# A two-layer mixer and a second block in one kernel: GpSimd's powers for the next layer spread over nine feed-forward units, and two weights' low parts put behind the attention's

## What is computed

```python
for layer in range(2):
    xn = rms_norm(h, attn_norm_g[layer])
    u_ssm, u_g, v_g, q, k, v = split(xn @ w_in[layer])
    y_ssm  = s5_mixer(u_ssm, ...)          # complex-diagonal state space model, GELU, GLU
    y_sgu  = spatial_gating(u_g, v_g, ...)
    y_diff = diff_attention(q, k, v, ...)  # differential attention, rms_norm at its end
    h = h + concatenate([y_ssm, y_sgu, y_diff]) @ w_out[layer]
    xn = rms_norm(h, ffn_norm_g[layer])
    h = h + (gelu(gate) * val) @ w_down[layer]   # gate, val: xn @ w_up after a causal conv of width 3
```

## Time and profile before

| | |
|---|---|
| median of 3 executions | 1001.0 us |
| lowest and highest | 999.23 and 1001.94 us |
| the profiled execution | 999.57 us |
| its span in the trace | 997.8 us |
| TensorE busy | 966.1 us |
| VectorE busy | 701.2 us |
| ScalarE busy | 547.1 us |
| GpSimd busy | 252.9 us |

### The profile page before, as it was taken

One profiled execution on the slowest core, in us unless ns is written; L12 is line 12 of the kernel. 1 busy time (PEld: TensorE's weight loads), 2 busy tenths in 40 slices (PEclk: granted clock), 3 DMA queues, 4 the chain that ended last, 5 costly groups with the idle time before them and its releaser, 6 DMA issues.

```text
span 997.8 us, 15915 instructions
## 1 busy us (share of the span) xinstructions
PE 966.1 (97%) x6214; PEld 848.8 (85%) x6214; DVE 701.2 (70%) x1072; ACT 547.1 (55%) x898; POOL 252.9 (25%) x196
## 2 busy tenths in 40 slices
PE   6989999999999999999999999999999999999997
PEld 4868789999888887889999988999877789888886
DVE  6998557798954688657677856547676755666785
ACT  7645546665654655645576545545354454555723
POOL 4890102688400021102525300003112300000030
PEclk9999999999999999999999999999999999999999
DMA  7622355655565553247666664665544545754462
GB/s 295 213 84 85 88 186 178 189 179 177 172 188 166 168 171 127 64 138 232 190 191 189 188 192 149 205 209 177 169 148 148 148 142 158 218 152 156 148 190 85
DMA packets 48474, 165.97 MB, mean 166 GB/s; under 512 B 6544, under 2 KB 7056, under 8 KB 48400
## 3 DMA queue, kind: packets, MB, share of 16 engines
q1 hardware_dynamic: 48400, 164.95, 53.2%
HBM read 162.83 MB, written 1.05 MB: 164 GB/s over the span
## 4 chain that ended last, share of the span: by engine, by line
PE 81%; DVE 13%; ACT 2%; issue 2%; POOL 1%; DMA 1%; SPq 0%; DVEq 0%; POOLq 0%; ACTq 0%
PE PJ L583 13%; PE PJ L585 12%; PE PJ L584 12%; PE PJ L576 9%; PE PJ L577 9%; PE PJ L578 9%; DVE wlo L1670 5%; PE PJ L539 2%; PE PJ L541 2%; PE PJ L540 2%; DMA raw<-weights_in 1%; PE T L1013 1%; PE PJ L700 1%; PE T L1004 1%; ACT whi L1072 1%
## 5 line engine op out<-in xcount | busy, mean ns | idle before, releaser
L1670 DVE TENSOR_TENSOR wlo<-raw,whi 128x1024 fp32r<-128x1024 f32 x294 | 375.2, 1308 | 92.1 <-ACT whi L1072 89.8
L1072 ACT ACTIVATE whi<-raw 128x1024 fp32r<-128x1024 f32 x294 | 303.3, 1062 | 67.8 <-DMA raw<-weights_in 61.3
L576 PE MATMUL PJ<-xthb,whi 128*128 128x256 f32 x864 | 243.2, 281 | 4.5 <-DVE wlo L1670 3.7
L578 PE MATMUL PJ<-xthb,wlo 128*128 128x256 f32 x864 | 242.1, 280 | 0.0
L577 PE MATMUL PJ<-xtlb,whi 128*128 128x256 f32 x864 | 242.0, 280 | 0.0
L583 PE MATMUL PJ<-whi,xthb 128*128 128x512 f32 (+1 forms) x432 | 175.2, 406 | 5.7 <-DVE wlo L1670 3.6
L576 PEld LDWEIGHTS PJ<-xthb,whi 128*128 128x128 f32 x864 | 163.1, 189 | 6.4 <-issue 6.2
L585 PE MATMUL PJ<-whi,xtlb 128*128 128x512 f32 (+1 forms) x432 | 167.8, 388 | 0.0
L584 PE MATMUL PJ<-wlo,xthb 128*128 128x512 f32 (+1 forms) x432 | 167.8, 388 | 0.0
L577 PEld LDWEIGHTS PJ<-xtlb,whi 128*128 128x128 f32 x864 | 163.1, 189 | 0.2
L578 PEld LDWEIGHTS PJ<-xthb,wlo 128*128 128x128 f32 x864 | 163.1, 189 | 0.0
(11 more groups left out here) (398 smaller groups left out, 1382.9 us busy)
## 6 DMA issues: line engine op xcount, KB each, us to landing
raw<-weights_in SPq DMA_DIRECT2D x294, 512.0 KB, 3.5
rt<-bmerge_in SPq DMA_DIRECT2D x6, 256.0 KB, 4.4
xres<-x_in SPq DMA_DIRECT2D x2, 512.0 KB, 5.5
xn<-mem_in SPq DMA_DIRECT2D x2, 512.0 KB, 5.7
y_out<-xn SPq DMA_DIRECT2D x4, 256.0 KB, 2.4
rowv<-rows_in SPq DMA_DIRECT2D x1, 576.0 KB, 10.2
ptmp<-bexp_in SPq DMA_DIRECT2D x2, 256.0 KB, 6.1
cex<-cexp_in SPq DMA_DIRECT2D x2, 256.0 KB, 8.2
```

The costliest lines, as they stand in the source:

```text
L576: pe.matmul(o, a, xh[:, k, :], start=(first and f % 2 == 0), stop=False, skip_group_check=True)
L578: m = pe.matmul(o, b, xh[:, k, :], start=False, stop=last, skip_group_check=True)
L1072: act.activation(whi[:, p % HIGHS, :], raw[:, p % LOADS, :], ACT.Copy).then_inc(hi_ready, 1)
L1670: dve.tensor_tensor(wlo[:, p % LOADS, :], raw[:, p % LOADS, :], whi[:, p % HIGHS, :].bitcast(F32), ALU.subtract).then_inc(lo_ready, 1)
```

## The change

There are two edits. GpSimd's input powers are cut into four steps, and the output powers into six, and these are put behind the products of units 2 to 5 and 7 to 9, with the folded coefficients behind unit 6. The two copies and the decay table stand behind unit 10. VectorE's turns move from behind unit 8's htl to behind the last unit's, and ScalarE's phase table from ahead of the last unit's hth to behind it. In the first layer only, two low parts move from ahead of the attention's `mix_low` calls to behind them.

```diff
--- before.py
+++ after.py
@@ -378,18 +378,21 @@
                 link(eng.tensor_tensor(t, i1, k1, ALU.mult))
                 link(eng.tensor_tensor(o, o, t, ALU.add))
 
-        def output_powers(eng, link, l, c, tmp):
+        def output_powers(eng, link, l, c, tmp, steps=(0, 1, 2)):
 
             ar, ai = (wide(apw[:, c, 1:STEP + 1, 8 * l:8 * l + 8].rearrange("p t s -> p s t"), 32, 3) for c in range(2))
             cr, nci = (wide(gpw[:, c, :, 0, :], STEP, 2) for c in range(2))
             t = tmp.rearrange("p (s t h) -> p s t h", s=ST, t=STEP)
             i0, k0, i1, k1, op = ((cr, ar, nci, ai, ALU.add), (nci, ar, cr, ai, ALU.subtract))[c]
             o = gpw[:, c, :, 1:STEP + 1, :]
-            link(eng.tensor_tensor(o, i0, k0, ALU.mult), False)
-            link(eng.tensor_tensor(t, i1, k1, ALU.mult))
-            link(eng.tensor_tensor(o, o, t, op))
-
-        def input_powers(eng, link, l, c, x, tmp):
+            if 0 in steps:
+                link(eng.tensor_tensor(o, i0, k0, ALU.mult), False)
+            if 1 in steps:
+                link(eng.tensor_tensor(t, i1, k1, ALU.mult))
+            if 2 in steps:
+                link(eng.tensor_tensor(o, o, t, op))
+
+        def input_powers(eng, link, l, c, x, tmp, steps=(0, 1)):
 
             ar, ai = (wide(apw[:, k, 1:STEP, 8 * l:8 * l + 8].rearrange("p t s -> p s t"), 32, 3) for k in range(2))
             br, bi = (wide(bex[:, k, :, :], STEP - 1, 2) for k in range(2))
@@ -397,11 +400,13 @@
             t = tmp[:, 0:ST * 96].rearrange("p (s t h) -> p s t h", s=ST, t=STEP - 1)
             o = xv[:, :, 1:STEP, :]
             i1, k1, op = (bi, ai, ALU.subtract) if c == 0 else (br, ai, ALU.add)
-            link(eng.tensor_copy(xv[:, :, 0, :], bex[:, c, :, :]), False)
-            link(eng.tensor_tensor(o, br if c == 0 else bi, ar, ALU.mult), False)
-            link(eng.tensor_tensor(t, i1, k1, ALU.mult))
-            link(eng.tensor_tensor(o, o, t, op))
-            eng.sem_inc(sem("xpow_ready"), 1)
+            if 0 in steps:
+                link(eng.tensor_copy(xv[:, :, 0, :], bex[:, c, :, :]), False)
+                link(eng.tensor_tensor(o, br if c == 0 else bi, ar, ALU.mult), False)
+            if 1 in steps:
+                link(eng.tensor_tensor(t, i1, k1, ALU.mult))
+                link(eng.tensor_tensor(o, o, t, op))
+                eng.sem_inc(sem("xpow_ready"), 1)
 
 
         @block.sync
@@ -1326,7 +1331,7 @@
                             hi_upto(end_pair(f"up{l}_{j}") + 5)
                     if j < UNITS:
                         unit_gelu(j)
-                    if l + 1 < LAYERS and j == UNITS - 1:
+                    if l + 1 < LAYERS and j == UNITS:
                         phase_tables(act, l + 1)
                 n_next = 2 if l + 1 < LAYERS else 5
                 if l + 1 == LAYERS:
@@ -1597,16 +1602,21 @@
                     if l + 1 == LAYERS and j == 6:
                         norm_rstd(4)
                     if l + 1 < LAYERS:
-                        if j in (3, 4):
+                        if j == 2:
                             pool.wait_ge(sem("bex_ready"), l + 2)
-                            input_powers(pool, link, l + 1, j - 3, x_tile(j - 3), ptmp)
-                        if j == 5:
+                        if 2 <= j < 6:
+                            input_powers(pool, link, l + 1, j // 2 - 1, x_tile(j // 2 - 1), ptmp, (j % 2,))
+                        if j == 6:
                             folded(l + 1)
-                        if j in (6, 7):
-                            output_powers(pool, link, l + 1, j - 6, ptmp)
+                        if j == 7:
+                            output_powers(pool, link, l + 1, 0, ptmp, (0, 1))
                         if j == 8:
+                            output_powers(pool, link, l + 1, 0, ptmp, (2,))
+                            output_powers(pool, link, l + 1, 1, ptmp, (0,))
+                        if j == 9:
+                            output_powers(pool, link, l + 1, 1, ptmp, (1, 2))
+                        if j == 10:
                             replicate_inputs(l + 1)
-                        if j == 10:
                             decay_table(pool, link, l + 1)
                             pool.sem_inc(sem("decay_ready"), 1)
 
@@ -1972,7 +1982,7 @@
                 lo_upto(s0 + 23)
                 diff_sums(1)
                 diff_norm(1)
-                lo_upto(s0 + 26)
+                lo_upto(s0 + (26 if l else 24))
                 mix_low(4, S1[:, :], 3)
                 mix_low(6, S0[:, :], 4)
 
@@ -2029,7 +2039,7 @@
                         lo_upto(end_pair(f"up{l}_{j}") + 4)
                     if j > 0:
                         unit_lo(j - 1)
-                    if l + 1 < LAYERS and j == 9:
+                    if l + 1 < LAYERS and j == UNITS:
                         dve.wait_ge(sem("gpow_ready"), 4)
                         phase_turns(dve, link, 1)
                     if l + 1 == LAYERS and j == 9:
```

## The result

The changed kernel takes 1001.29 us (median of 12 runs, 999.78 to 1003.78) where the kernel before, timed beside it, takes 999.88 (12 runs, 999.22 to 1002.19). The ratio of the two is 1.0016, with an interval of 1.0008 to 1.0023: slower by about 1.6 us, which lies within the 0.3% that the forecast called no change. The profiled execution has a span of 998.8 us, against 997.8. Most lines of the changed kernel stand five to ten further down (1072 has become 1077, 1670 is 1680, 1859 is 1869, 1297 is 1302, 649 is 654, 583 is 588), and this execution is 0.5 us ahead of the one before from its first rows on.

A forecast was written before the change was run, and what follows sets the result against it. TensorE, busy 966.1 of 997.8 us, was taken to bound the kernel. The terms -1.5 - 3.35 + 2.45 + 2.6 gave +0.2 us; with the shown runs' median of 1001.0 the forecast was 1001.2 us, range 998.0 to 1004.6.

The forecast's parts named there:

- Its own signs of being wrong: Wrong if a new wait is missing or over 3.5 us, or the granted clock falls at either.
- the wait for xtlb: TensorE's wait for the attention output's low half at the first mixing end was to be under 0.3 us.
- the short wait at the sixth pair: First down projection: a short TensorE wait after the fifth pair's 2.7 us, with ScalarE's table ahead of its release.
- Mixing end, -1.5: First mixing end: one low part instead of three ahead of the attention parts releases TensorE 1.5 us earlier (1.2 to 1.6).
- Units 8 and 9, -3.35: First layer's feed-forward units: moved GpSimd powers lie beside VectorE's taps, removing the whole 3.35 us loss.
- the bound of -3.0: Units 8 and 9: the gain is only 3.0 us if one low part is still caught.
- the third rival: Units 8 and 9: powers never slowed the low parts, so 3.35 us stays; +3.5 us, 1004.5 us, 3 in 100.
- Transposes, +2.45: Second eight input transposes behind unit 6: TensorE waits for GpSimd's late powers, a new 2.45 us stall (2.0 to 2.8).
- The rival by which the engines take turns after every instruction: VectorE and GpSimd alternate, so the transposes' stall is 0.9 instead of 2.45 us; 999.7 us, 12 in 100.
- the rival with both waits hidden: Transposes and turns cost the path nothing: -4.85 us, 996.2 us, 6 in 100.
- Phase table and turns, +2.6: First down projection: later turns and phase table delay TensorE's fifth and sixth pairs, +2.6 us (2.1 to 3.2).
- TensorE's clock falls in the new stalls: At transposes and down projection, 1.65 us lost per fall: one gives 1002.8 us (10 in 100), two 1004.4 (4 in 100).

The follow-up runs named there:

- the mixing end alone: The kernel before with only VectorE's low parts reordered at the first mixing end: 999.04 us, ratio 0.9990.
- the kernel filled at both: The changed kernel with TensorE's waits at the input transposes and the down projection filled with transposes of the identity: 1000.52 us, ratio 1.0005.
- the powers alone: The changed kernel with the first mixing end's low parts ordered as in the kernel before: 1003.75 us, ratio 1.0038.
- the kernel without the transposes' wait: The changed kernel with the last two instructions of GpSimd's second set of input powers issued in unit 4, not unit 5: 998.87 us, ratio 0.9989.
- The third set of the changed kernel: The changed kernel timed and profiled a third time, unchanged, beside the kernel before: 1000.46 us, ratio 1.0015.
- the positions mended: The changed kernel with those input powers finished in unit 4 and the splits ahead of turns and phase tables: 994.46 and 995.15 us.
- the kernel filled at the down projection: The changed kernel with sixteen transposes of the identity between the down projection's fourth and fifth pairs: 1000.91 us, ratio 1.0012.

## Why the prediction was right, point by point

**The forecast of 1001.2 us** met 1001.29, partly by luck. Its sum was +0.2 us and 1.4 to 1.6 was measured; the level it was put on, the median of three runs at 1001.0, was 1.1 over the 999.88 of twelve runs.

**Its own signs of being wrong.** One of them came true. By its last sentence the prediction is wrong if the granted clock falls at either new wait, and it fell at the down projection (0.52 and 0.62 in the windows above). Of the rest, the wait for xtlb was met (0.44 us on the weight load, none in the matmul's own row), the new waits are 2.13 and 2.35 where about 2.4 and 2.7 were named, and the short wait at the sixth pair is missing in this profile. So the terms and the places were right, and the picture of a kernel that keeps its clock was not.

**Mixing end, -1.5.** The weight load moved from 120.20 to 118.16, of which 0.54 is this execution's head start: -1.50. The edit alone was timed at 1.0 and 0.9.

**Units 8 and 9, -3.35.** Measured -3.25 and -0.10. The 0.10 had nothing to do with the powers: the second profile of before and the mixing end alone have 11.20 and 11.21 us at that step. The reason given was half right. The powers don't lie beside the taps alone: two low parts are still caught (238.26), more than the one that the bound of -3.0 allowed for, and yet TensorE waits for none, because the loss on VectorE is 2.6 us (4.92 - 2 x 1.16) and not 8.6. With the steps at 11.20 us the third rival (3 in 100) is out.

**Transposes, +2.45.** Measured +2.33, with the released instruction and the engine as named. Moving the two powers one unit up took 2.7 us out. The rival by which the engines take turns after every instruction (12 in 100) is out too: gtd of unit 5 took 5.55 us (209.11), and the powers ended at 218.03. So is the rival with both waits hidden (6 in 100).

**Phase table and turns, +2.6.** Without a fall of the clock 2.64 was measured (the kernel filled at both; 16.68 - 14.05 = 2.63 in the powers alone). The chain was as described, down to the short second wait at the sixth pair (0.48), which is ScalarE's chain. Putting the splits ahead took it out whole. In the changed kernel's own profile the term is 3.62, since the clock fell.

**The sum** of the four as measured is -1.50 - 3.35 + 2.33 + 2.64 = +0.12 us, with the clock kept up (+0.22 without the 0.10 above). The kernel with both waits filled is that case: 1000.52 against 1000.13, a ratio of 1.0005 whose interval takes in +0.12 us.

**What was mis-sized is the rival "TensorE's clock falls in the new stalls"**, at 10 in 100 for one fall and 4 in 100 for two. The price was right where the transposes' fall is concerned: 1.65 forecast, 1.55 and 1.60 measured; the other costs 0.98. The chance was wrong: four profiled executions had both waits bare, and three of them show one fall and the fourth both. With 3 in 6 and 4 in 5 as the chances, the mean cost is 0.5 x 1.6 + 0.8 x 1.0 = 1.6 us, and 0.12 + 1.6 = 1.7 is what the three timings of the changed kernel show (1.6, 2.3 and 1.5 by the ratios; by the means of the single times 1.1, 2.1 and 1.6). The forecast of two falls has a slip besides: 0.2 + 2 x 1.65 is 3.5, not 3.4. The step that failed was the sentence that the point of decision "lies between" a wait of 1.5 and one of 3.15 us, followed by a forecast as if 2.45 lay below it. There is no sharp point in these traces: 2.11 and 2.40 us drew a fall and 2.15 and 2.36 drew none. Nor did the very wait that I had taken as proof of a fall always draw one. 12 of the 14 profiles have it with 3.14 to 3.16 us; the clock fell behind it in nine and kept up in three. In two of those three it fell only behind a second wait of 1.8 us, 5 us later. The third is the kernel without the transposes' wait, whose timeline of TensorE and windows have:

```profile
71.69 0.47 PE L588 MATMUL PJ<-whi,xthb 128*128 128x512 f32 x1 [3.14 <-DVE wlo L1680]
...
76.49 0.47 PE L588 MATMUL PJ<-whi,xthb 128*128 128x512 f32 x1 [1.79 <-DVE wlo L1680]
```

```profile
70.00:72.00 2.00, 0.31 (x1) 0.30 (x2) 2.00 (x2) 0.49 (x1) 1.92 (x2) 1.00 0.02 6
72.00:74.00 2.00, 2.00 (x10) 1.65 (x9) 1.90 (x5) 0.14 (x1) 1.80 (x2) 1.00 0.00 0
```

The first matmul took 0.47 us and not 0.77, and the clock stayed at 1.00. By the Trainium skill (TensorE: Matmul & The Clock Gate, Part 1, "What's actually happening") the monitor's phase is not tied to the kernel's start and the cold stretch differs from run to run; the traces fit that, as the same code at the same wait went both ways.

The price of 1.65 us was met by luck too. It is the clock time lost in a stretch where the fall cost the path nothing: from that matmul to the attention's transposes (their weight load at 116.20 in before) it is 45.59 us in before, with a fall, and 117.28 - 71.69 = 45.59 in the kernel above, without one, because TensorE then waits 1.79 us for the next low part instead. Behind the transposes nothing covers a fall, and there the price was 1.55 and 1.60 us.

The single times are weaker evidence. The third set of the changed kernel has seven times from 1000.23 to 1000.81 us, at a mean granted clock of 0.995, and four from 1002.45 to 1003.80, at 0.992 or 0.993, with nothing between; the gap of 1.64 us is near the price of the transposes' fall. But the widest gaps in the other two sets are 0.8 and 1.3 us, and one execution at 0.992 took 999.78 us. So this is argued from one set, not shown.

**Where the gain went.** The change took out 4.85 us of waiting and put 4.97 back at two places that it had itself made late, and these two drew 1.6 us more in clock. The idea was sound and two of its positions were not: with the positions mended the same edits are worth 4.5 us. That is a little under the 4.85, and the marks show where some of it stays: the step over the transposes is 13.06 us there and not 12.96, and the three units behind it take 11.31, 11.30 and 11.31, so 0.4 us go to the slower pitch of the last section.

## What to carry to other kernels

Before work is spread over earlier or later slots, list for each piece who reads it first and which long instruction now stands ahead of it; one slot earlier for two instructions, and splits ahead of a wait and not behind it, made the difference between +1.6 and -4.5 us here. A wait of 2 us or more on TensorE should be priced with a fall of its clock at even odds or worse (7 of 11 here, and 9 of 12 at 3.15 us), not left out because the likeliest execution lacks it. And a fall has its full price only where TensorE would not have waited anyway: the one at 70 us cost nothing here. Where the wait can't be removed, harmless transposes in it kept the clock in all three profiled executions, and cost nothing.

## What the runs showed of the hardware

**A fall is a matter of chance, and transposes count against it.** 11 bare waits of 2.1 to 2.4 us drew 7 falls, 3 filled ones none, and the timings of the kernel filled at both are lower than the changed kernel's by 1.8 us in their own set (ratios 1.0005 and 1.0023). If 7 in 11 were the chance with the filling too, three without a fall would come about once in 20 times. Length counts for something, but not sharply: 12 waits of 1.47 to 1.79 us near 59 us drew no fall, and in the kernel filled at the down projection one of 3.16 us drew none where one of 1.83 us, 5 us later, was followed by one. The Trainium skill (TensorE: Matmul & The Clock Gate, Part 4) says that transposes don't count as busy time in the same way; three executions and one timing speak against that for holding a clock that is already up. Raising it with transposes was not tried.

**Two pitches at full clock.** At a granted clock of 1.00 a unit of 96 matmuls takes either 11.20 or 11.31 us (116.7 or 117.8 ns for each). The slower one appeared in the first layer behind the transposes (units 8 to 10) in all four profiles in which the moved powers leave no wait there, but not in the two of before and the one of the mixing end alone, which have no wait there either (before has it in one step of its first profile). It appeared in all ten units of the second layer in three of 14 profiles, one of them of the changed kernel, which has 11.20 in its other two, and in the first step of the first layer in six of the 14. What sets it stays open.

**The first 117 us scatter more than the rest.** The kernel filled at the down projection ran the same instructions as the changed one until there and was 2.53 us later at the weight load of the attention's transposes (118.19 against 115.66 us). Of this, 0.9 came before the first projection, and 1.6 from a fall of the clock at 76 us that nothing covered; the changed kernel's own fall, at 70, was covered. A difference of two single profiles under 2.5 us is therefore read from marks on either side of the place, not from the spans.
